# A mixture-of-experts encoder: expert rows added to the residual in DRAM by one indirect DMA a block, and reloaded

## The reference

```python
def _hier_moe(h, w_group, b_group, w_expert, b_expert, w1, w3, w2):
    # top-1 of 4 groups, then top-2 of its 8 experts: expert_id, gate per token
    ...
    def expert_block(args):
        xblk, e = args
        return (jax.nn.silu(xblk @ w1[e]) * (xblk @ w3[e])) @ w2[e]

    yb = lax.map(expert_block, (xb, blk_e)).reshape(P, D)
    y = jnp.zeros((N, D), dtype=h.dtype).at[buf_tok].add(yb * buf_w[:, None], mode='drop')
    return y.reshape(B, S, D)

    # in reference(), for each layer:
    x = x + _hier_moe(h, ...)
```

## Time and profile before

| | us |
|---|---|
| median of 3 runs | 1918.59 (1916.19 to 1924.55) |
| the profiled execution | 1923.78 |
| its span, first to last instruction | 1922.0 |
| PE busy | 1511.0 (79%) |
| ACT busy | 567.2 (30%) |
| DVE busy | 537.3 (28%) |
| POOL busy | 220.7 (11%) |

### The profile page before, as it was taken

One profiled execution on the slowest core, in us unless ns is written; L12 is line 12 of the kernel. 1 busy time (PEld: TensorE's weight loads), 2 busy tenths in 40 slices (PEclk: granted clock), 3 DMA queues, 4 the chain that ended last, 5 costly groups with the idle time before them and its releaser, 6 DMA issues.

```text
span 1922.0 us, 23884 instructions
## 1 busy us (share of the span) xinstructions
PE 1511.0 (79%) x8622; PEld 873.3 (45%) x8623; DVE 537.3 (28%) x1079; ACT 567.2 (30%) x1060; POOL 220.7 (11%) x272
## 2 busy tenths in 40 slices
PE   6966667598876886886399988785987998878992
PEld 4832235244443443443278743462544554444551
DVE  3488743310000000000433387433100110000113
ACT  4445544122111111111232267621211222112222
POOL 1156510000000000000200010000000000000001
PEclk9987788699998998998699999987999999899996
DMA  3550004699999999999332210067999999999994
GB/s 139 198 197 1 0 22 151 232 348 379 384 380 381 385 377 381 384 379 360 137 107 92 84 39 20 22 239 267 370 382 381 379 369 373 385 379 380 379 378 160
DMA packets 206939, 499.57 MB, mean 260 GB/s; under 512 B 7560, under 2 KB 8584, under 8 KB 206896
## 3 DMA queue, kind: packets, MB, share of 16 engines
q1 hardware_dynamic: 183920, 438.70, 62.6%
q0 software_dynamic: 11200, 39.85, 6.4%
q10 hardware_dynamic: 11776, 20.46, 2.8%
HBM read 465.92 MB, written 33.06 MB: 260 GB/s over the span
## 4 chain that ended last, share of the span: by engine, by line
PE 43%; SPq 30%; DVE 11%; issue 6%; DMA 5%; ACT 4%; POOL 1%; POOLq 0%; DVEq 0%; ACTq 0%
SPq L399 19%; PE bank L353 15%; PE bank L682 11%; SPq L404 10%; PE bank L696 6%; DMA w<-in_w 4%; DVE sg L1031 3%; PE bank L599 2%; DVE P L1075 1%; PE bank L540 1%; PE bank L485 1%; PE bank L662 1%; PE bank L579 1%; DVE mx L1083 1%; PE bank L626 1%
## 5 line engine op out<-in xcount | busy, mean ns | idle before, releaser
L682 PE MATMUL bank<-w,xT 128*64 128x256 f32 x4480 | 542.8, 404 | 148.8 <-DMA w<-in_w 143.2
L682 PEld LDWEIGHTS bank<-w,xT 128*64 128x64 f32 x4480 | 343.4, 146 | 375.5 <-issue 242.7
L1304 DVE TENSOR_TENSOR hh<-bank,sgate 64x256 f32<-64x256 f32 x140 | 59.6, 426 | 956.9 <-ACT sgate L933 956.9
L696 PE MATMUL bank<-w,hT 128*64 128x512 f32 x1120 | 271.2, 605 | 25.7 <-ACT hT L936 25.7
L933 ACT ACTIVATE sgate<-bank 64x256 f32<-64x256 f32 x140 | 52.7, 376 | 443.2 <-PE bank L682 441.6
L1387 POOL COPY icol<-idxI 64x1 uint32 x72 | 12.9, 179 | 1008.3 <-DVE xT L1297 946.4
L696 PEld LDWEIGHTS bank<-w,hT 128*64 128x64 f32 x1120 | 67.9, 136 | 120.0 <-issue 80.0
L933 ACT ACT_TABLE_LOAD x70 | 89.8, 1283 | 110.4 <-issue 110.4
L328 DVE TENSOR_TENSOR wlo<-raw,whi 128x512 fp32r<-128x512 f32 (+1 forms) x112 | 74.6, 680 | 170.6 <-ACT whi L320 170.5
L320 ACT ACTIVATE whi<-raw 128x512 fp32r<-128x512 f32 (+1 forms) x112 | 66.8, 614 | 165.6 <-PE bank L353 165.2
L353 PE MATMUL bank<-whi,hi 128*128 128x512 f32 x224 | 92.7, 414 | 17.1 <-DVE wlo L328 16.1
(11 more groups left out here) (217 smaller groups left out, 1635.9 us busy)
## 6 DMA issues: line engine op xcount, KB each, us to landing
w<-in_w SPq DMA_DIRECT2D x192, 2048.0 KB, 21.7
y_dram<-ysb ACTq DMA_DIRECT2D x140, 128.0 KB, 6.2
raw<-in_od_w_in SPq DMA_DIRECT2D x12, 1024.0 KB, 5.2
y_dram<-zeros POOLq DMA_DIRECT2D x2, 4096.0 KB, 18.8
raw<-in_ev_w_in SPq DMA_DIRECT2D x6, 1024.0 KB, 5.3
raw<-in_ev_w_out SPq DMA_DIRECT2D x4, 1024.0 KB, 5.1
hn_dram<-HN POOLq DMA_DIRECT2D x2, 2048.0 KB, 14.2
raw<-in_od_w_out SPq DMA_DIRECT2D x4, 1024.0 KB, 5.1
```

What stands on the lines that cost most here:

```text
L682: last = pe.matmul(B[(1, 4)[c]][j * SLOT:j * SLOT + SLOT, 0:HH], xT[:, k, :], W13[s][:, j, k, c * HH:c * HH + HH], start=k == 0, stop=k == ...
L696: last = pe.matmul(B[3][j * SLOT:j * SLOT + SLOT, :], hT[:, k, :], W2[s][:, k, j * 512:j * 512 + 512], start=k == 0, stop=k == FK - 1)
L1304: dve.tensor_tensor(hh[:, c * HH:c * HH + HH], B[(1, 4)[c]][SLOT:P, 0:HH], sgate[SLOT:P, c * HH:c * HH + HH], ALU.mult).then_inc(s_h[l], 1)
```

## The change

`y_dram`, `YG`, `sloti` and the combine go. The router also builds, for each slot of each block, its gate (`gate`) and its destination row (`rowI`), by 24 more small products and a few DVE operations. SP stores `X` to `x_dram`, seen as rows of 512 columns, before each expert stage. ACT scales by the gate in the eviction. POOL then adds the 128 half rows of `ysb` to their rows of `x_dram` by one indirect DMA that accumulates in DRAM; since one addition must have landed before the next may start, ACT's eviction and POOL wait for the one before (`s_yst`). After the last one SP reloads `X` by four DMAs, and the norm waits for those. Slots without a token point at 64 rows of zeros behind the tokens.

```diff
@@ SP, before and after the expert stage
+            def reload_x(l, tot):
+                sp.wait_ge(s_yst[l], 16 * tot + 16)
+                for t in range(TT):
+                    sp.dma_start(X[:, t, :], x_dram[l][2 * t * P:2 * (t + 1) * P, :].rearrange("(p j) n -> p (j n)", j=2)
+                                 ).then_inc(s_x[t], 16)
...
                 load_w13(l, 1, 1)
+                sp.wait_ge(s_mix[l], 2 * TT)
+                sp.dma_start(x_dram[l][0:2 * T, :].rearrange("(t p j) n -> p t (j n)", p=P, j=2), X[:, :, :]).then_inc(s_xst, 16)
                 sp.wait_ge(s_hnst, 16 * l + 16)
...
             sp.wait_ge(s_g2[1], tot)
+            reload_x(1, tot)
@@ PE, end of the router
+                pe.wait_ge(s_gsel, l + 1)
+                for j in range(8):
+                    pe.matmul(B[6][0:SLOT, 0:NBLK + 1], slotsel[:, j, :], blkg[:, j, :], start=j == 0, stop=j == 7)
+                    pe.matmul(B[6][SLOT:P, 0:NBLK + 1], slotsel[:, j, :], blkg[:, j, :], start=j == 0, stop=j == 7)
+                for j in range(8):
+                    last = pe.matmul(B[7][SLOT:P, 0:NBLK + 1], slotsel[:, j, :], blkt[:, j, :], start=j == 0, stop=j == 7)
+                last.then_inc(s_gidx, 1)
@@ ACT, end of a block
-                    act.wait_ge(s_yst[l], 32 * b + 1)
-                    act.activation(ysb[:, :], B[3][:, :], ACT.Copy).then_inc(s_yev[l], 1)
-                    act.wait_ge(s_yev[l], b + 2)
-                    for j in range(2):
-                        act.dma_start(y[bass.ds(b, 1), :, j * 512:j * 512 + 512].rearrange("b s n -> (b s) n"),
-                                      ysb[j * SLOT:j * SLOT + SLOT, :]).then_inc(s_yst[l], 16)
+                    act.wait_ge(s_yst[l], 16 * b + 16)
+                    act.activation(ysb[:, :], B[3][:, :], ACT.Copy, scale=gate[:, bass.ds(b, 1)]).then_inc(s_yev[l], 1)
...
-            rms(4, lambda t: (s_mo[1], 2 * (t + 1)))
+            rms(4, lambda t: (s_x[t], 48))
@@ DVE
-            def combine(l):
...
@@ POOL, the expert stage
-                with pool.Fori(0, more) as b:
+                def gather(b):
                     pool.wait_ge(s_xT[l], b + 1)
...
-                pool.wait_ge(s_yst[l], 32 * tot + 1)
...
-                for j in range(2 * TT):
-                    pool.indirect_dma_start(out=YG[:, j, :], out_offset=None, in_=y_dram[l],
-                                            in_offset=bass.IndirectOffsetOnAxis(ap=sloti[:, j:j + 1], axis=0)).then_inc(s_yg[j], 16)
+                gather(0)
+                pool.wait_ge(s_row, l + 1)
+                pool.wait_ge(s_xst, 16 * l + 16)
+                with pool.Fori(0, tot) as b:
+                    gather(pool.snap(b + 1))
+                    pool.wait_ge(s_yst[l], 16 * b + 16)
+                    pool.tensor_copy(rcol[:, :], rowI[:, bass.ds(b, 1)]).then_inc(s_rcol[l], 1)
+                    pool.wait_ge(s_xst, 16 * l + 16)
+                    pool.wait_ge(s_rcol[l], b + 1)
+                    pool.wait_ge(s_yev[l], b + 2)
+                    pool.indirect_dma_start(out=x_dram[l], out_offset=bass.IndirectOffsetOnAxis(ap=rcol[:, :], axis=0),
+                                            in_=ysb[:, :], in_offset=None, compute_op=ALU.add).then_inc(s_yst[l], 16)
```

More of the change, by code:

```diff
@@ L175, in build @@
         blksel = tl.take("blksel", [P, 8, NBLK + 1])
+        blkt = tl.take("blkt", [P, 8, NBLK + 1])
+        blkg = tl.take("blkg", [P, 8, NBLK + 1])
         sm = Region(small_at, 8 * KB)
@@ L208, in build @@
         wgt = keep2.take("wgt", [P, TT, 2])
-        sloti = keep2.take("sloti", [P, 8], U32)
         idxI = keep2.take("idxI", [SLOT, NBLK + 1], U32)
         icol = keep2.take("icol", [SLOT, 1], U32)
-        passed = keep2.take("passed", [P, 1])
+        rowf = keep2.take("rowf", [P, NBLK + 1])
+        rowI = keep2.take("rowI", [P, NBLK + 1], U32)
+        gate = keep2.take("gate", [P, NBLK + 1])
+        rcol = keep2.take("rcol", [P, 1], U32)
         blkf = keep2.take("blkf", [P, NE + 1])
@@ L219, in build @@
         B = [ctx.enter_context(nc.psum_tensor(f"bank{i}", [P, 512], F32)) for i in range(8)]
-        hn_dram = [nc.dram_tensor(f"hn_dram{l}", (T, D), F32, kind="Internal").ap() for l in range(DEPTH)]
-        y_dram = [nc.dram_tensor(f"y_dram{l}", (NBLK * SLOT, D), F32, kind="Internal").ap() for l in range(DEPTH)]
+        hn_dram = [nc.dram_tensor(f"hn_dram{l}", (T + SLOT, D), F32, kind="Internal").ap() for l in range(DEPTH)]
+        x_dram = [nc.dram_tensor(f"x_dram{l}", (2 * (T + SLOT), D // 2), F32, kind="Internal").ap() for l in range(DEPTH)]
         line_dram = nc.dram_tensor("line_dram", (8, REL), F32, kind="Internal").ap()
@@ L277, in build @@
         s_mv = sems2("s_mv")
-        s_yg = [sem(f"s_yg_{j}") for j in range(2 * TT)]
-        s_all = sem("s_all")
-        s_mo = sems2("s_mo")
+        s_rcol, s_gsel, s_gidx, s_row, s_xst = sems2("s_rcol"), sem("s_gsel"), sem("s_gidx"), sem("s_row"), sem("s_xst")
         s_out, s_cbf, s_y0 = sem("s_out"), sem("s_cbf"), sem("s_y0")
@@ L435, in _ @@
                     sp.wait_ge(s_y0, 32)
+                    for q in range(DEPTH):
+                        sp.wait_ge(s_yst[q], 16)
                 else:
@@ L650, in router @@
                 for j in range(8):
-                    last = pe.matmul(B[5][0:SLOT, 0:NBLK + 1], slotsel[:, j, :], blksel[:, j, :], start=j == 0, stop=j == 7)
+                    last = pe.matmul(B[5][0:SLOT, 0:NBLK + 1], slotsel[:, j, :], blkt[:, j, :], start=j == 0, stop=j == 7)
                 last.then_inc(s_idx, 1)
+                pe.wait_ge(s_gsel, l + 1)
[5 more added lines that the diff above has]
+                last.then_inc(s_gidx, 1)
             def experts(l):
@@ L912, in router @@
                 act.wait_ge(s_y0, 32)
+                for q in range(DEPTH):
+                    act.wait_ge(s_yst[q], 16)
                 for k in range(1, KD, 2):
@@ L927, in experts @@
                 act.activation(r4[:, 11, :], r4[:, 4, :], ACT.Copy).then_inc(s_yev[l], 1)
-                act.activation(r4[:, 10, :], r4[:, 4, :], ACT.Copy).then_inc(s_yst[l], 1)
-                y = y_dram[l].rearrange("(b s) d -> b s d", s=SLOT)
+                act.wait_ge(s_row, l + 1)
                 with act.Fori(0, tot) as b:
@@ L1184, in router @@
                 dve.wait_ge(s_y0, 32)
+                for q in range(DEPTH):
+                    dve.wait_ge(s_yst[q], 16)
                 for k in range(0, KD, 2):
@@ L1383, in experts @@
                 pool.wait_ge(s_hnst, 16 * l + 16)
-                more = pool.snap(tot + 1)
-                with pool.Fori(0, more) as b:
+                def gather(b):
                     pool.wait_ge(s_xT[l], b + 1)
-                    pool.tensor_copy(icol[:, :], idxI[:, bass.ds(b, 1)]).then_inc(s_icol[l], 1)
+                    pool.tensor_copy(icol[:, :], idxI[:, bass.ds(b, 1)] if not isinstance(b, int) else idxI[:, b:b + 1]).then_inc(s_icol[l], 1)
                     pool.wait_ge(s_hnst, 16 * l + 16)
```

44 lines of the change are left out of this document (23 added, 21 removed).

## The result

The changed kernel takes 2125.64 us (median of 4 runs, 2117.55 to 2130.54) beside 1919.62 for the kernel before: 1.107 times as long (95% interval 1.102 to 1.111). The forecast was 1973, its range ended at 2085. The direction was right, the size was not: +206 us instead of +54.

What follows compares the result with a forecast made beforehand. Loads set layer 0's pace (17.9 us a block), PE much of layer 1's (13.0). Late gather +50, addition +20, joints -18.5, router +3 gave +54.5 on 1918.6: 1973 us, range 1903 to 2085.

Steps and rivals of the forecast that it cites:

- Step 1: Expert stages: the gather behind the scatter on POOL lands late, PE waits 3.3 us a block; layer 1 +50 us.
- X: Time from one eviction's end to the next row transposes on PE; forecast 10.0 us against 6.7 at PE's pace.
- sign of being wrong: Profile after, layer 1: a granted clock of 0.5 inside most blocks would show the forecast wrong.
- rival of the clock: PE's mid-block wait lowers the granted clock, adding 2 to 2.7 us a block: pace 18.5, about 2060 us; chance 0.11.
- the loop hides there under the loads: Layer 0's expert stage: load pace of 17.9 us is above the loop's 16.3, so the late gather doesn't show.
- Step 2: The store becomes an addition in DRAM: 0.7 us a block more, +20 us in layer 0, not counted in layer 1.
- Step 3: Joints, from a layer's last eviction to the norm's last square: shorter by 9 and 9.5 us.
- Step 4: Router: 24 more small products a layer and the store of X delay the first gather; +3 us over both layers.
- A second turn: The gather waits some 3 us more behind the scatter's rows in POOL's queue: 12.6 us, middle 2075 us; chance 0.17.
- The gather is not late: Expert stages: the gather lands 4 us after issue, PE doesn't wait; 1903 us if the addition is free; chance 0.22.

Runs made afterwards that it cites:

- after_filled: The changed kernel with 14 products into an unread bank on PE ahead of its wait for the gathered rows; 2019.31 us (1.0515).
- before_late2: The kernel before, gathers from the third on held until the eviction two blocks earlier, plus two POOL multiplications, no scatter or addition; 2110.91 us (1.100).
- gather_ahead: The changed kernel with POOL issuing the gather of block b+2 ahead of the addition of block b; 1937.97 us (1.0097).
- ahead_plain: The changed kernel with gathers issued ahead of the scatter, and a scatter that overwrites instead of adding; 1900.9 us (0.9898).

## Why the prediction was wrong

**Step 1, the late gather: right in mechanism, and wrong in what it costs.** The gather into `xg` became the head of PE's waits. X was forecast at 10.0 us and came out at 10.2 and 10.5 in the median. Two of its terms were off and made up for each other: the way from the eviction's end to the gather's issue is 3.4 us (513.18 to 516.54), not 2.55, because the adding scatter holds POOL for 1.58 us and not 0.95; the landing is 6.8, so the 0.5 us behind the scatter's rows is not seen. That X came out so near is in part luck. X costs layer 1 64 us (+50 in the sum, within its bounds) and nothing in layer 0, as said.

The step that failed is the next one: "PE waits 3.3 us in each block that ran at its own pace, and the pace becomes 16.3 us". That adds the wait to a block whose second half still takes 6.3 us. It takes 9.0 and 8.4 in the mean. The sign of being wrong that the forecast named, a clock of 0.5 inside most blocks of layer 1, is there: 29 of its 37 second halves are slow. The forecast saw this possibility as its rival of the clock, and had the rows for it: a fall after 6.2 us, none after 1.6. A wait of 3.3 us lay between the two, and I gave it 0.11. The expert stages of the kernel before have no row that is nearer (PE's waits for weights are under 2.3 or over 6.0 us), but its mixers have, and the forecast left them out. In layer 1's mixer of that kernel PE stands still for 3.63 us behind products that follow one another, and the same products take 0.63 us behind the wait, for 0.39 ahead of it:

```profile
1244.21 0.39 PE L353 MATMUL bank<-whi,lo 128*128 128x512 f32 x1
1248.22 0.79 PE L353 MATMUL bank<-whi,hi 128*128 128x512 f32 x1 [3.63 <-DVE wlo L328]
...
1249.24 0.63 PE L353 MATMUL bank<-whi,lo 128*128 128x512 f32 x1
```

The granted clock, in the columns of the earlier trace rows, is 1.00 ahead of that wait and 0.50 behind it:

```profile
1240.50:1244.50 4.00, 4.00 (x19) 3.03 (x17) 0.00 (x0) 3.96 (x4) 0.00 (x0) 1.00 0.00 0
1248.20:1251.20 3.00, 2.98 (x7) 2.40 (x8) 1.77 (x3) 0.61 (x2) 0.00 (x0) 0.50 0.17 13
```

In layer 0's mixer, where PE does little, two waits of 3.23 us went both ways (the clock behind them is 1.00 at 143.0 us and 0.70 at 150.7). These rows would have given this rival a far larger chance. The pace that this rival named for layer 1, 18.5 us, is the measured one (18.52). Its total, 2060, was too low by 65 us, most of it because it left layer 0 out: with the slow half the loop is at 19.44 there, above the loads' 17.9, and "the loop hides there under the loads" no longer holds. after_filled shows both halves of that: with the clock held, layer 0 is hidden again, and layer 1 runs at 17.39, 1.1 above the forecast's 16.3, as the scatter's 1.58 us, a landing of 7.7 us and the eviction's 0.69 make it.

What is shown and what is argued: that lateness alone does it is shown by before_late2, and that a busy PE gives 106 us back by after_filled. That the clock, and not some other effect of an idle PE, slows the products is read from the granted clock: 0.50 in the windows, and in the mean 0.51 to 0.79 in each slow half and 1.00 in each other.

**Step 2, the addition: right where loads set the pace.** +20 us in layer 0 was forecast, 16 was measured in gather_ahead's order; 0.7 us a block, 0.8 measured. In the change's own order the loop sets the pace of layer 0, so its 21 us come another way, and their nearness to 20 is luck: X is 9.5 us in the mean without the addition, 10.4 with it. The Trainium skill (Collectives: The Full Stack, "The bandwidth ceiling") has the reduce step of a collective, an addition in the DMA engines, at half a copy's rate, for its two source reads. POOL's queue agrees with that rate: ahead_plain's 124 us for 41.95 MB are 0.78 us for the 0.26 MB of a plain scatter, and the addition puts 0.8 on top. That ACT "scales in the eviction itself; it waits for PE anyway, so nothing" was a small miss: the eviction takes 0.69 instead of 0.60 us, and the second half is 6.45 instead of 6.27 even at the full clock; in a loop that goes through the eviction this is on the path, some 12 us over 68 blocks.

**Step 3, the joints: right.** -9.1 and -7.7 us against -9.5 and -9. Their two pieces are as forecast: the last addition lands 7.3 and 4.7 us after its issue (7 and 4.5 in the sum), the last reload 7.6 and 8.5 us after the first one's issue (7.5).

**Step 4, the router: wrong by 6 us.** +3 was forecast, -3.1 measured over both mixers and routers; where it comes from stays open.

**The rivals.** "A second turn" is out: its X of 12.6 us is not seen, and without the addition X is still 9.7 us in layer 1. The Trainium skill (DMA: Bandwidth & Descriptors, "Queues, rings and completion order") has the rule that spoke for it, an engine that drains a whole packet of one ring before it turns to the next. No run here shows the wait of a further round: in layer 0 of after_filled, where the engines are full (share 1.05 from 445 to 900), the gather behind a scatter lands in 6.8 us, no later than in the kernel before (6.9). In its layer 1, at a share of 0.95, it takes 7.7, and why stays open. "The gather is not late" would have needed a landing of 4 us; none of the stages had that as its median.

**The sums.** Three of the forecast's smaller sums don't come out, and none bears on the miss: a pace of 15.3 makes layer 1's lower bound +16 and not +25; the second turn with a wait of 2 us is some +22 in layer 0 and not +30; the gather in time with 0.7 us for each of 70 blocks is 1952 and not 1945.

## What to carry to other kernels

When an edit makes PE wait in the middle of a block, the wait is not the price: read in the trace what the granted clock does behind waits of that length, and add the products that follow at the lower clock. Look for them in all stages of the trace, not only in the one that changes. Where no row has a wait of that length, that term belongs in the sum's bounds with a large chance. It also decides whether a stage that looks hidden under another pace stays hidden. And of two DMAs on one engine, the one that a later block waits for goes first: the same work in the other order on POOL was 188 us faster.

## What the runs showed of the hardware

An adding indirect DMA of 128 rows of 2 KB holds POOL for 1.58 us, the same one without addition for 1.01 to 1.02:

```profile
L1419 POOL DMA_INDIRECT x_dram<-ysb,rcol x70: 1562/1577/1619, 392.1 to 1911.0; - x70
```

```profile
L1419 POOL DMA_INDIRECT x_dram<-ysb,rcol x69: 998/1017/1030, 393.6 to 1880.1; - x69
```

(first of gather_ahead, then of ahead_plain). It lands after a median of 8.0 us (layer 0 of gather_ahead; 8.2 in the changed kernel) against 6.5. And idle work has a value: 14 products whose result nobody reads, 3.2 us of PE's time in a block, made the changed kernel 106 us faster.
